# Fourteen projection blocks of a layer, multiplied in pairs by seven block products ahead of the prompt attention

## The reference

```python
mod = jax.nn.silu(c) @ lp['w_ada'] + lp['b_ada']
h = rms_norm(x, lp['norm_pre_g']) * (1 + scale[:, None]) + shift[:, None]
proj = jnp.einsum('bld,de->ble', h, lp['w_in'])
q_down, kv_down, k_rope, mla_gate, rw_in, rw_gate, gm_u, gm_v, gm_gate = split_last(proj, IN_SPLITS)
q = jnp.einsum('blr,rhd->blhd', rms_norm(q_down, lp['q_norm_g']), lp['w_uq'])
ckv = rms_norm(kv_down, lp['kv_norm_g'])
o_mla = attend(q_nope, q_pe, ckv, kpe, lp['w_uk'], lp['w_uv'])       # 4 heads, causal on the prompt
o_rw, wkv_new, shift_new = rwkv7_time_mix(rw_in, shift0, wkv0, lp)
o_gm, vn = chunk_gmlp(gm_u, gm_v, lp)                                # vn: layer norm of gm_v with gain and bias
out = jnp.einsum('ble,ed->bld', concat(silu(gates) * (o_mla, o_rw, o_gm)), lp['w_out'])
y = x + gate[:, None] * rms_norm(out, lp['norm_post_g'])
```

## Time and profile before

| | |
|---|---|
| median of three runs | 1952.89 us |
| profiled execution, first to last instruction | 1938.0 us |
| what lies around the span, against the median | 14.9 us |
| TensorE busy | 1833.1 us, 95% |
| VectorE, ScalarE, GpSimd busy | 894.3, 512.0, 181.6 us |
| first layer: main block on TensorE | 56.91 to 609 us |

### The profile page before, as it was taken

How to read it: one execution, slowest core, us unless ns; L and a number is a source line. 1 busy time by engine, 2 the same in 40 slices (tenths; PEclk the granted TensorE clock), 3 DMA queues, 4 the chain that set the end, 5 groups by cost and what they waited for, 6 DMA issues and landing times. The chain is left out here.

```text
span 1938.0 us, 45850 instructions
## 1 busy us (share of the span) xinstructions
PE 1833.1 (95%) x19344; PEld 1141.3 (59%) x19344; DVE 894.3 (46%) x1985; ACT 512.0 (26%) x1186; POOL 181.6 (9%) x175
## 2 busy tenths in 40 slices
PE   3999999999999899999969999999999989999998
PEld 2565666666665566654436656766666656666543
DVE  2125124223495678765230340332325857777642
ACT  3111122223331333432221110222224223343221
POOL 0010000002330300000000200000023321000000
PEclk9999999999999999999989999999999999999999
DMA  9600000000023666643155000010001147665441
GB/s 376 249 12 28 22 22 22 22 22 22 23 68 100 190 202 195 191 173 147 69 203 208 1 28 22 22 33 22 11 22 39 52 131 209 193 203 149 187 167 41
DMA packets 105543, 198.66 MB, mean 103 GB/s; under 512 B 17410, under 2 KB 87580, under 8 KB 101620
## 3 DMA queue, kind: packets, MB, share of 16 engines
q1 hardware_dynamic: 105332, 195.67, 30.6%
HBM read 182.81 MB, written 21.26 MB: 105 GB/s over the span
## 5 line engine op out<-in xcount | busy, mean ns | idle before, releaser
L825 PE MATMUL PB<-RB,R 128*128 128x344 f32 x1632 | 493.2, 455 | 0.0
L825 PEld LDWEIGHTS PB<-RB,R 128*128 128x128 f32 x1632 | 302.0, 190 | 156.4 <-issue 15.2
L1689 PE MATMUL PB<-WUQ,Q 32*32 32x256 f32 x5120 | 199.0, 385 | 20.1 <-DVE WUQ L1870 12.0
L2074 PE MATMUL PB<-RB,R 128*128 128x512 f32 x496 | 214.9, 593 | 0.0
L1870 DVE STREAM_TRANSPOSE WUQ<-RB 128x512 f32<-128x512 f32 x316 | 203.4, 680 | 17.8 <-DMA RB<-in_cache 14.2
L2074 PEld LDWEIGHTS PB<-RB,R 128*128 128x128 f32 x496 | 93.9, 190 | 115.9 <-issue 113.8
L985 ACT ACTIVATE R<-PB 128x344 f32<-128x344 f32 x90 | 41.3, 458 | 401.8 <-PE PB L825 401.8
L1240 DVE TENSOR_TENSOR PB<-PB,CST 128x128 f32<-128x128 f32 x64 | 18.8, 295 | 222.0 <-PE PB L845 222.0
L1689 PEld LDWEIGHTS PB<-WUQ,Q 32*32 32x32 f32 x5120 | 90.0, 104 | 43.9 <-issue 27.7
L673 PE MATMUL PB<-RB,R 128*128 128x344 f32 x288 | 85.4, 460 | 1.8 <-PEq L250 1.8
L1122 DVE COPY R<-PB 128x320 f32<-128x320 f32 x16 | 7.9, 492 | 146.7 <-PE PB L684 146.7
(11 more groups left out here) (367 smaller groups left out, 2617.5 us busy)
## 6 DMA issues: line engine op xcount, KB each, us to landing
RB<-in_cache SPq DMA_DIRECT2D x512, 160.0 KB, 2.6
R<-in_w_in SPq DMA_DIRECT2D x44, 512.0 KB, 3.8
R<-in_w_ada SPq DMA_DIRECT2D x14, 1536.0 KB, 9.7
RB<-in_w_ada SPq DMA_DIRECT2D x6, 1536.0 KB, 16.6
RB<-out_x_stream SPq DMA_DIRECT2D x2, 4096.0 KB
out_x_stream<-RB SPq DMA_DIRECT2D x16, 512.0 KB
RB<-in_x_prompt SPq DMA_DIRECT2D x1, 4096.0 KB
RB<-in_w_out SPq DMA_DIRECT2D x8, 512.0 KB, 3.8
```

Source lines behind the costliest of these rows:

```text
L825: mm = pe.matmul(jobbank(j)[:, 0:CH], ring[:, blkno[n] % 4, k, :], hT[:, k, chunk(c)], start=(k == 0), stop=(k == KT - 1))
L1689: mm = pe.matmul(PB[qp[o], 2 * (h % 2) + q % 2, 0:256], Q4[qp[q], g, :], k[qp[q], c], start=(g == 0), stop=(g == NB - 1), skip_group_check ...
L2074: mm = pe.matmul(PB[0:n, 2 * (t % 2) + hf, :], mixT[:, k, cols(t)], wo[:, k, hf * 512:(hf + 1) * 512], start=(k == 0), stop=(k == 5))
```

## The change

Two neighbouring blocks are taken as one product of a weight matrix (2 x 2 tiles of 512 features by 128 columns) and the activations (2 x 2 tiles of 512 features by 516 tokens). Instead of eight products of tiles it makes seven, with sums and differences of tiles before and after (the scheme of Strassen in Winograd's form). The differences of the activations, T1 to T4, are made once a layer by VectorE during the latents; those of the weights, S1, S2 and S4, once a pair. Each of the seven products is done in two halves of 258 columns. The 14 blocks q, g and rw go this way, in seven pairs; the key and value latents come before them, and everything else of the list (query projections, keys, values, attention) after them. So the jobs left as filler are the gv, gg, gu and rg blocks: 4 halves in the head of the attention, 14 between its steps, 36 after it. `VN` and the 18 GpSimd operations move behind the attention. The latents' weights are loaded in the first block, the DMA of `wuk` and `wuv` comes later, and several tiles get other places in SBUF. The row scaling of the latents (ckv) moves from the query stage into the pairs.

```diff
@@ constants, block order and views
+NPAIR = 7
+HT, QT = T // 2, T // 4
 BLOCKS = ([(f"q{i}", i * 128, 128) for i in range(3)]
           + [(f"g{i}", 704 + i * 128, 128) for i in range(4)]
-          + [(f"gv{i}", 2624 + i * 128, 128) for i in (1, 0)]
           + [(f"rw{i}", 1216 + i * 128, 128) for i in range(7)]
+          + [(f"gv{i}", 2624 + i * 128, 128) for i in range(2)]
...
+        B11, B12 = hT[:, 0:4, 0:HT], hT[:, 0:4, HT:T]
+        B21, B22 = hT[:, 4:8, 0:HT], hT[:, 4:8, HT:T]
...
+            pairbank = lambda x, s: PB[:, 3 * s + x, 0:QT]
...
-            JOBS = [(f"g{i}", c) for i in range(4) for c in range(3)] + [("gv", t) for t in range(9)] \
-                + [("rw0", 0), ("gvs", 0), ("rw0", 1), ("rw0", 2)] + [(f"rw{i}", c) for i in range(1, 7) for c in range(3)] \
+            JOBS = [("gv", 8), ("gvs", 0)] + [("gv", t) for t in range(8)] \
                 + [(n, c) for n in ("gg0", "gg1", "gu0", "gu1", "rg0", "rg1") for c in range(3)]
@@ the plan that TensorE, ScalarE and VectorE follow
-            feed(18)
+            feed(2)
             plan += [("warm", 0, 0), ("S", 0, 0), ("MX", 0, 0), ("MX", 1, 0)]
-            feed(6)
+            feed(2)
             plan += [("EX", 0, 0), ("EX", 1, 0), ("NO", 0, 0), ("NO", 1, 0)]
             left = len(halves) - 36
...
                 plan.append(("PV", u, 0))
-                if 10 <= u < 13:
-                    plan.append(("VN", u - 10, 0))
                 feed(share[3])
-            plan += [("mix", 6, 0), ("mix", 2, 0), ("mix", 3, 0), ("kg", 0, 0), ("kg", 1, 0)]
+            plan += [("mix", 6, 0), ("mix", 2, 0), ("mix", 3, 0), ("VN", 0, 0), ("VN", 1, 0), ("VN", 2, 0), ("kg", 0, 0), ("kg", 1, 0)]
@@ TensorE
-                    for f in range(3):
-                        project(f"q{f}")
+                    def product(w, b, x, s, first):
+                        for k in range(4):
+                            mm = pe.matmul(pairbank(x, s), w[:, k, :], b[:, k, s * QT:(s + 1) * QT], start=(first and k == 0), stop=(k == 3),
+                                           skip_group_check=True)
+                        return mm
+                    def pair(m):
+                        i, j = 2 * m, 2 * m + 1
+                        W0, W1 = ring[:, i % 4], ring[:, j % 4]
+                        pe.wait_ge(win_in[i % 4], 16 * (i // 4 + 1))
+                        for s in range(2):
+                            if m:
+                                pe.wait_ge(st_act, 4 * m - 1 + s)
+                            product(W0[:, 0:4], B11, 0, s, True).then_inc(st_full, 1)
+                        pe.wait_ge(sum_done, 2 * m + 2)
+                        for s in range(2):
+                            if m:
+                                pe.wait_ge(st_dve, 10 * m - 3 + s)
+                            product(S2, T2, 1, s, True).then_inc(st_full, 1)
+                        for s in range(2):
+                            pe.wait_ge(st_act, 4 * m + 1 + s)
+                            product(W0[:, 4:8], B21, 0, s, False).then_inc(st_full, 1)
+                        for s in range(2):
+                            pe.wait_ge(st_dve, 10 * m + 1 + s)
+                            product(W1[:, 0:4], T3, 1, s, False).then_inc(st_full, 1)
...
+                            product(S1, T1, 2, s, True).then_inc(st_full, 1)
...
+                            product(W1[:, 4:8], T4, 1, s, False).then_inc(st_full, 1)
...
+                            product(S4, B22, 2, s, False).then_inc(st_full, 1)
...
+                    for m in range(NPAIR):
+                        pair(m)
@@ ScalarE: the first product and the finished first quarter are copied out; then squares, scales or SiLU of whole blocks
+                    def first(m):
+                        for s in range(2):
+                            act.wait_ge(st_full, 14 * m + 1 + s)
+                            act.activation(part(2 * m + 1, 0, s), pairbank(0, s), ACT.Identity).then_inc(st_act, 1)
...
+                            if n[0] == "q":
+                                act.activation(qsq[:, f, :], qd[:, f, :], ACT.Square)
+                                act.activation(qd[:, f, :], qd[:, f, :], ACT.Identity, scale=vec[:, V_QN + f:V_QN + f + 1]).then_inc(qg_done, 1)
+                            elif n[0] == "g":
+                                act.activation(mixT[:, f, :], mixT[:, f, :], ACT.Silu).then_inc(qg_done, 1)
@@ VectorE: sums of weights, and ten additions of 258 columns a pair
+                    def weight_sums(m):
...
+                        dve.tensor_tensor(S1, W1[:, 0:4], W1[:, 4:8], ALU.add)
+                        dve.drain()
+                        dve.tensor_tensor(S2, S1, W0[:, 0:4], ALU.subtract)
+                        dve.tensor_tensor(W1[:, 0:4], W0[:, 0:4], W1[:, 0:4], ALU.subtract).then_inc(sum_done, 1)
...
+                    def pair(m):
...
+                            dve.tensor_tensor(part(i, 1, s), pairbank(1, s), part(j, 0, s), ALU.add).then_inc(st_dve, 1)
...
+                        if t == 0:
+                            dve.tensor_tensor(T1, B12, B11, ALU.subtract)
@@ GpSimd: the gain and bias of the gMLP rows
-                    pool.wait_ge(vn_dve, 1)
-                    for t in range(9):
-                        pool.tensor_tensor(vraw[:, t], vraw[:, t], lng, ALU.mult)
-                    pool.drain()
-                    for t in range(9):
-                        gain = pool.tensor_tensor(vraw[:, t], vraw[:, t], lnb[:], ALU.add)
-                    gain.then_inc(vn_done, 1)
...
                     for o, j in enumerate(MIX):
+                        if o == 5:
+                            pool.wait_ge(vn_dve, 1)
+                            for t in range(9):
+                                pool.tensor_tensor(vraw[:, t], vraw[:, t], lng, ALU.mult)
...
                         if o >= 2:
                             pool.wait_ge(mx_done, o - 1)
@@ SyncE, first block and main block
                     sp.wait_ge(ada_used, 2)
+                    sp.dma_start(wkv_in, dram("w_kv").rearrange("p (k c) -> p k c", k=KT)).then_inc(s_wkv, 16)
+                    sp.wait_ge(ada_used, 3)
...
+                        if i < 2 * NPAIR + 4:
+                            sp.wait_ge(st_full, 14 * (i // 2 - 1))
```

More of the change, by code:

```diff
@@ L275, in _ @@
                         pe.wait_ge(s_pre[k], 16)
-                        mm = products(k, range(6 if k == 0 else 4), False)
-                        if k == 0:
+                        mm = products(k, range(6 if k < 2 else 4), False)
+                        if k < 2:
                             mm.then_inc(ada_used, 1)
@@ L298, in _ @@
                     mm.then_inc(shift_full, 1)
-                    for k in (1, 2):
-                        products(k, (4, 5), False)
+                    products(2, (4, 5), False)
                     pe.wait_ge(am_done, 1)
@@ L664, in free_small @@
                             pe.wait_ge(sm_free, smlno[n] - 1)
-                    def project(n):
-                        i = blkno[n]
-                        free_big(n)
-                        pe.wait_ge(win_in[i % 4], 16 * (i // 4 + 1))
-                        for k in range(KT):
-                            for c in range(3):
-                                mm = pe.matmul(bigbank(n)[:, c, :], ring[:, i % 4, k, :], hT[:, k, c * CH:(c + 1) * CH],
-                                               start=(k == 0), stop=(k == KT - 1))
-                        mm.then_inc(big_full, 1)
@@ L753, in _, with keys @@
                                      ident[0:rows(t), 0:rows(t)]).then_inc(sm_full, 1)
-                    pe.wait_ge(s_w, 16 * 13)
+                    pe.wait_ge(s_w, 16 * 11)
+                    pe.wait_ge(s_wkv, 16 * 3)
                     pe.wait_ge(sm_free, smlno[("kt", 8)] + 1)
-                    for h in range(H):
+                    def keys(h):
                         free_big(f"k{h}")
@@ L762, in _ @@
                         mm.then_inc(big_full, 1)
+                    keys(0)
+                    keys(1)
                     free_small("qabs", 0)
@@ L774, in _ @@
                     mm.then_inc(sm_full, 1)
+                    keys(2)
+                    keys(3)
                     def query_columns():
@@ L811, in project @@
                             if n == "gv":
-                                w2 = ring[:, bass.ds(0, 2, step=3), k, :]
+                                w2 = ring[:, 2:4, k, :]
                                 if c < NT:
@@ new lines, in first, with whole @@
+                    def first(m):
+                        for s in range(2):
+                            act.wait_ge(st_full, 14 * m + 1 + s)
+                            act.activation(part(2 * m + 1, 0, s), pairbank(0, s), ACT.Identity).then_inc(st_act, 1)
+                    def whole(m):
+                        for s in range(2):
+                            act.wait_ge(st_full, 14 * m + 5 + s)
```

(22 more changed lines are left out.)

275 lines of the change are left out of this document (172 added, 103 removed).

## The result

The changed kernel takes 1981.47 us, the median of four runs (1979.53 to 1983.66), against 1952.99 us before (four runs, 1949.55 to 1953.24): a ratio of 1.0146, 95% interval 1.0131 to 1.016. The forecast was 1977 us. So the 14.9 us that the table of the profile before calls "around the span" are not around it: the profiled execution of before was some 13 us shorter than its timed runs, whose spans must lie near 1951 us. Over the experiments the kernel before had medians of 1941 to 1953 us from one group of runs to the next.

A forecast was written before the change was run, and what follows sets the result against it. TensorE's list plus its gaps was taken as the bound, busy 1833.1 of 1938.0 us. Per layer -23.7 + 26 + 8 + 1.7 = 12.0 us, 24 for two: span 1962, time 1977 us, range 1943 to 2005 (8 in 10).

The forecast's parts named there:

- The products: Fourteen blocks' matmuls on TensorE: 194.6 us a layer become 170.9 in seven pairs, 0.436 us per 258-column matmul, saving 23.7.
- rival 4: In the pairs: each half product pays a handoff, 9.8 us more a layer, 1997 us; chance 0.05.
- The sums and loads: Beside the pairs and latents: VectorE's additions and the weight loads stay hidden, 0 us; bounds 0 to 10 and 0 to 3.
- The attention: Attention without its filler: gaps of 28.3 us a layer against 2.45 before, so a cost of 26 us.
- The lower bound of 16 us: Attention gaps if all 16 halves cover fully and each unit hides half a microsecond more: 28.3 - 10 - 2.5.
- Behind the attention: Stage from token shifts to `kr`: moved VN and GpSimd work delays the bonus units by 8 us a layer; bounds 0 and 12.4.
- The sum by exclusion: Behind the attention: VectorE's and GpSimd's work added as if mutually exclusive, 50.2 us, so `kr` starts 9.1 us late.
- Rival 3: Behind the attention: GpSimd's operations find idle time, 8 us less a layer, 1961 us; chance 0.16.
- The clock: TensorE's granted clock falls once a layer, costing 1.7 us; bounds 0 to 6 falls.
- Rival 2: In the attention: the clock falls six times a layer, 8.5 us more than taken, 1994 us; chance 0.14.
- Rival 1: Attention gaps only 12 us instead of 28, 1940 us; the change wins below 16.5 us a layer; chance 0.16.
- The base: Timed runs taken to stand 14.9 us above the profiled span, unchanged, so a 1962 us span becomes 1977.

The follow-up runs named there:

- e3: Changed kernel with VN back in the attention, gain and bias beside it, and the 14 gv halves in the first ten units; ratio 1.0048 to before.
- e4: Changed kernel with five pairs instead of seven, rw3 to rw6 as jobs in the attention, VN in units 10 to 12; ratio 0.9887 to before.
- e6: Changed kernel with six pairs instead of seven, rw5 and rw6 as jobs in the attention, VN in units 10 to 12; ratio 0.9961 to before.
- e1: Kernel before with 46 job halves moved ahead of the first scores, so 14 of 60 remain between the attention's steps; no pairs; ratio 1.0326 to before.
- e9: Changed kernel with its 14 gv halves spread evenly over the units, none behind the product with the values; ratio 1.0033 to before.
- e10: The six-pair kernel e6 with its 26 halves spread evenly over the units, none behind the product with the values; ratio 0.9832 to before.
- e7: Kernel before with VN behind the attention and only the last of GpSimd's 18 gain and bias operations kept; ratio 1.0016 to before.
- e2: Kernel before with only VN and GpSimd's 18 gain and bias operations moved behind the attention; ratio 1.0096 to before.
- e8: Changed kernel with eight useless matmuls in each of the 12 units without a job half ahead of the values; ratio 1.0163 to before.

## Why the prediction was right, and where it was off

The direction and the mechanism held; the forecast was 4.5 us low. By the medians the change costs 14.2 us a layer, against 12.0 forecast. In the profiles the stages of layer 1, block start to decode, grew by 16.9 us (554.07 to 570.95) and those of layer 2 by 15.4 (555.75 to 571.19). The two profiled executions also differ outside these stages: by 4.4 us from the decode of layer 1 to the blocks of layer 2 (403.0 to 407.4) and by 5.7 behind the start of the decode of layer 2. The first of these stretches takes 398.7 us in e3 and 401.9 in e4 with the code of the changed kernel, the second 368.8 and 364.7, so I put this part down to the executions and not to the change.

- **The products, -23.7.** Right: 7 x (24.36 - 27.8) = -24.1 (e4 to e6). 258 columns cost 0.435 us (24.36 / 56), which is the slope's 0.436, and no half product paid a handoff, so rival 4 has no support.
- **The sums and loads, 0.** Right: no idle time within the pairs, and the rest of the front is within 1 us.
- **The attention, +26.** Measured +30.8 and +30.1, of it 3 to 4 for the clock: the gaps are 27. That the missing filler makes them is shown (e1). Unit by unit the chain was close in part: units without a half ahead of the values idled 3.0 us (the first), 3.05 (the seventh) and 2.1 (the fifteenth), where 2.8, 3.3 and 2.5 were forecast. The eighth and ninth idled 2.2 and 1.8 against 3.3 and 2.3. A part of each gap is not in the idle column: eight turns are 0.9 us by the pace of 0.113 us, and their row has 1.06, so it ends 0.16 us after the pace would have it. That halves behind the values cover little was the right idea; the placing was worth more than the sum gave it (e9, e10). The lower bound of 16 us was not what its own words add up to: half a microsecond more in each of 16 units is 8 us, and they were not taken off.
- **Behind the attention, +8.** Measured +8.7 of wait (10.59 - 1.93). The stage is 10.5 to 11.5 us longer (122.42 and 123.39 against 112.5, with a first half that is 0.6 shorter), since the clock is at half for 10 to 14 us around that wait. The largest part is GpSimd's operations (e7). The sum by exclusion put `kr` at 50.3 us behind the attention's end (548.8 - 498.5), and it came at 49.3. Rival 3 falls. But two errors of the sum nearly cancel, and that it came within 1 us is in part luck. One step failed: the chain was to start 0.1 us behind the attention's end (498.6), with the wait for the shift DMA gone. GpSimd's power of the last gv job (507.70) stands ahead of its shifts, so they start 5.3 us behind it, and VectorE's first 7.4. From the first of these shifts (509.71) to `kr` the chain then took 44 us instead of 50.2, so some 6 us of the two engines' work did overlap. e2, which keeps the DMA wait, waits nearly as long as the changed kernel (10.0 and 10.6). (The terms of the sum before add up to 34.5 and not 34.7, which changes nothing.)
- **The clock, +1.7.** The step "I take one fall a layer" failed. Each layer has two or three low stretches in the attention, 10.2 us at half, and one of 10 to 14 us at the bonus wait. By the 3 to 4 us of e8 and the 1.8 to 2.8 by which the last stage grew more than its wait, I estimate 5 to 7 us instead of 1.7. Rival 2 was half true: the clock fell often, but not six times, and by e8 this was worth at most 4 us in the attention, where the rival named 8.5 more than the forecast. This is most of what the forecast lacked.
- **Rival 1** (gaps of only 12 us) falls by e1; its break-even of 16.5 us a layer was well below the 27 measured.
- **The base.** "The runs stand 14.9 us above the span, and nothing changes around it" was wrong as a statement, as shown above; adding the forecast growth to the median was sound all the same.

The Trainium skill, page "SBUF — State Buffer", section "SBUF: two separate sides", has the port pair as a lock held for a whole instruction, for VectorE with two SBUF inputs against GpSimd. The trace agrees: scans of 64 columns take 0.26 us alone, 0.76 beside GpSimd's operations of 0.73, and the one beside a shift of 1.90 takes 1.93. The Trainium skill, page "TensorE: Matmul & The Clock Gate", section "A second HAM failure mode: psum-queue depth-cycling", says that short idles between groups of matmuls, if they come often enough, make the clock swing. e8 agrees, since useless work in the same idles kept it at 1.00. In e6 an attention with 15.9 us of such idles stayed at 1.00 too.

## What to carry to other kernels

Filler work in a latency-bound stage is worth what it covers, so before taking it out, add up the gaps that it hides: here 27 us a layer, against 24 us that fewer products saved. Keep as much of it as closes the gaps and put every piece between the producer and the wait that ends last; five pairs with placed filler gained 2.2% where seven without lost 1.5%. And check which stage a displaced step lands in: 12 us of GpSimd work that cost nothing beside the attention cost 7 us beside VectorE's chain.

## What was unexpected of the hardware

- Dummy products in TensorE's short waits kept its granted clock at 1.00 over 163.7 us in which, without them, it was 0.97 in the mean; they gained no time, as each cost up to 0.7 us where the wait was shorter.
- Beside each other the operations of VectorE and GpSimd here took about the time of the longer one, so the shorter one pays. VectorE's scans of 0.26 us took 0.76 beside GpSimd's gains and biases, which took their usual 0.73, and 1.93 beside a shift of 1.90. GpSimd's nine gains took 9.10 us instead of 6.19; the long ones, up to 1.71 us, stood beside VectorE's shifts of 1.75, and those beside scans took 0.72.
- Stages with the same code differ by 9 us and more between profiled executions: 398.7 us (e3) to 407.4 (changed) from the decode of layer 1 to the blocks of layer 2, and 364.7 (e4) to 378.2 (e9) from the decode of layer 2 to the end. So a single profile's span is no base for a forecast of the median.
